# A two-layer decoder on one core: the order of VectorE and ScalarE at the beginnings and ends of feed-forward blocks

## The reference

```python
def swiglu(x, wgu, wd):
    gate, up = jnp.split(x @ wgu, 2, axis=-1)
    return (jax.nn.silu(gate) * up) @ wd

for i in range(DEPTH):                                   # DEPTH = 2
    h = h + 0.5 * swiglu(rms_norm(h, ffn1_norm[i]), ffn1_wgu[i], ffn1_wd[i])   # D_FF = 2816
    ...                                                  # mixing and cross attention
    h = h + 0.5 * swiglu(rms_norm(h, ffn2_norm[i]), ffn2_wgu[i], ffn2_wd[i])
return rms_norm(h, final_norm)
```

## Time and profile before

| | |
|---|---|
| median of 3 runs | 2177.72 us (2177.59 to 2182.73) |
| the profiled execution | 2179.78 us, its span 2177.8 us |
| TensorE busy | 2127.3 us, 98% |
| TensorE weight loads | 1855.7 us, 85% |
| VectorE busy | 1502.1 us, 69% |
| ScalarE busy | 907.6 us, 42% |
| GpSimd busy | 138.7 us, 6% |

### The profile page before, as it was taken

The page is one execution under the profiler, slowest core; times in us unless marked ns, Lnnn a source line. Parts: engine busy times, 40 slices in busy tenths (PEclk is TensorE's granted clock), DMA queues, the critical chain, the costliest instruction groups (busy, mean ns, idle before and its releaser), DMA issues. The chain is left out here.

```text
span 2177.8 us, 30026 instructions
## 1 busy us (share of the span) xinstructions
PE 2127.3 (98%) x12251; PEld 1855.7 (85%) x12251; DVE 1502.1 (69%) x2194; ACT 907.6 (42%) x1305; POOL 138.7 (6%) x114
## 2 busy tenths in 40 slices
PE   7999999999999999999989999999999999999998
PEld 6889888888888879888878888978888888888886
DVE  7777775657664787777577776756586457777775
ACT  6333433435434533334344433334464345334332
POOL 0000001100020200000110000021001102000001
PEclk9999999999999999999999999999999999999999
DMA  4333332422221233333223333343132212332331
GB/s 137 116 107 102 90 111 82 135 96 79 97 97 58 87 99 102 105 103 98 87 87 116 88 110 104 97 131 99 62 117 98 78 58 84 121 103 90 107 102 54
DMA packets 267940, 211.96 MB, mean 97 GB/s; under 512 B 7358, under 2 KB 234268, under 8 KB 267804
## 3 DMA queue, kind: packets, MB, share of 16 engines
q1 hardware_dynamic: 264544, 205.55, 30.3%
q10 hardware_dynamic: 3260, 4.51, 0.8%
HBM read 207.93 MB, written 2.10 MB: 96 GB/s over the span
## 5 line engine op out<-in xcount | busy, mean ns | idle before, releaser
L1804 PE MATMUL ps<-hid_hi,wn_hi 128*128 128x512 f32 x592 | 232.5, 393 | 2.5 <-DVE wn_lo L1355 1.8
L1805 PE MATMUL ps<-hid_lo,wn_hi 128*128 128x512 f32 x592 | 231.3, 391 | 0.0
L1806 PE MATMUL ps<-hid_hi,wn_lo 128*128 128x512 f32 x592 | 230.4, 389 | 0.0
L1366 DVE SCALAR_TENSOR_TENSOR h<-ps,h 128x512 f32<-128x512 f32 x224 | 148.3, 685 | 88.2 <-PE ps L1806 85.3
L1805 PE MATMUL ps<-hn_lo,wn_hi 128*128 128x512 f32 x448 | 175.2, 391 | 0.0
L1804 PE MATMUL ps<-hn_hi,wn_hi 128*128 128x512 f32 x448 | 175.1, 391 | 0.0
L1806 PE MATMUL ps<-hn_hi,wn_lo 128*128 128x512 f32 x448 | 174.2, 389 | 0.0
L638 ACT ACTIVATE w_hi<-raw 128x2048 fp32r<-128x2048 f32 x61 | 116.7, 1913 | 118.3 <-PE ps L1806 95.0
L1804 PE MATMUL ps<-hn_hi,w_hi 128*128 128x512 f32 x384 | 152.5, 397 | 3.5 <-DVE w_lo L1168 2.0
L780 ACT ACTIVATE wn_hi<-raw 128x768 fp32r<-128x768 f32 (+1 forms) x104 | 81.2, 806 | 170.8 <-PE ps L1806 170.8
L1805 PE MATMUL ps<-hn_lo,w_hi 128*128 128x512 f32 x384 | 150.7, 393 | 0.0
(11 more groups left out here) (323 smaller groups left out, 5897.7 us busy)
## 6 DMA issues: line engine op xcount, KB each, us to landing
raw<-in_ffn_wgu_dram SPq DMA_DIRECT2D x174, 512.0 KB, 4.8
raw<-in_ffn_wd_dram SPq DMA_DIRECT2D x48, 512.0 KB, 3.7
raw<-in_ffn_wd_dram SPq DMA_DIRECT2D x80, 256.0 KB, 3.7
raw<-in_w_in_dram SPq DMA_DIRECT2D x40, 512.0 KB, 4.4
raw<-in_cross_wkv_dram SPq DMA_DIRECT2D x32, 512.0 KB, 3.8
raw<-in_w_out_dram SPq DMA_DIRECT2D x16, 512.0 KB, 4.0
raw<-in_cross_wq_dram SPq DMA_DIRECT2D x16, 512.0 KB, 3.8
raw<-in_cross_wo_dram SPq DMA_DIRECT2D x16, 512.0 KB, 3.9
```

What stands on the lines that cost most here:

```text
L1366: dve.scalar_tensor_tensor(out=h[:, m, :], in0=ps[:, down_bank(c, m), :], scalar=0.5, in1=h[:, m, :], op0=ALU.mult, op1=ALU.add).then_inc( ...
L1804: pe.matmul(dst, a_hi, b_hi, start=start, stop=False)
L1805: pe.matmul(dst, a_hi, b_lo, start=False, stop=False)
L1806: return pe.matmul(dst, a_lo, b_hi, start=False, stop=stop)
```

## The change

It moves work on VectorE and ScalarE at both ends of the feed-forward blocks; no operation is added or left out. In a block's beginning the readouts of tiles 0 and 1 go ahead of the sums of pairs (tile 0 only in the first block, where it came behind pairs 0 and 1), N3's rounding and low part go behind tile 2's readout and between additions, and DB 0 is loaded ahead of N3. At a block's end the next stage's first unit is rounded and split ahead of squares and low parts, and each low part stands one addition later. In the last block TensorE asks for one scaled tile fewer before m = 6 and turns the one left out behind the last matmul. The down weights of chunk 1 get four places of their own (quarter_at), with other waits. One address of mg_lo moves by 128 bytes.

```diff
 def ffn_order():
-    order = [("N", 0), ("N", 1), ("N", 2), ("DA", 0), ("N", 3), ("DB", 0), ("S", 0), ("DA", 1)]
+    order = [("N", 0), ("N", 1), ("N", 2), ("DA", 0), ("DB", 0), ("N", 3), ("S", 0), ("DA", 1)]
...
+        def quarter_at(p, tiles):
+            return p * 512 if tiles == 2 else (p % 2) * 768
...  (ScalarE)
                 def down_round(c, p):
-                    if p < 2:
+                    if p < 2 or (c, p) == (1, 2):
                         act.wait_ge(wn_used, late_no(F, c + 2))
+                    elif c == 1:
+                        act.wait_ge(n_done, late_no(F, 3))
                     else:
                         act.wait_ge(d_done, d_no(F, c, 2 * p - 3))
...
                     round_third()
+                    whole_silu(0)
+                    whole_hid(0)
                 pair_scaled(0)
                 pair_scaled(1)
                 pair_rounded(0)
...
                     round_third()
                     copy_rb(rb_no, 7)
-                whole_silu(0)
-                whole_hid(0)
+                    whole_silu(0)
+                    whole_hid(0)
+                act.wait_ge(w_used, base + 4)
+                slot_round("DA", 0, 1, 1024)
+                whole_silu(1)
+                whole_hid(1)
                 pair_scaled(2)
                 pair_scaled(3)
                 pair_rounded(2)
                 pair_rounded(3)
-                act.wait_ge(w_used, base + 4)
-                slot_round("DA", 0, 1, 1024)
-                whole_silu(1)
-                whole_hid(1)
-                whole_round(3, 0)
-                whole_round(3, 1)
                 act.wait_ge(w_used, base + 5)
                 slot_round("DB", 0, 0, 1024)
                 whole_silu(2)
                 whole_hid(2)
+                whole_round(3, 0)
+                whole_round(3, 1)
...
+                if not final:
+                    round_next(0)
                 act.wait_ge(form_ready, 2 * fast_no(F, FAST - 1))
                 for m in range(KT):
...
-                    if m == 3 and not final:
-                        round_next(0)
...  (VectorE)
+                def first_hid():
+                    slot_low(3, "N", 2, 0, 2048)
+                    dve.wait_ge(rb_ready, L * 3 + (1 if f == 0 else 3))
+                    whole_gate(0)
+                    whole_scale(0)
+                    whole_product(0)
+                    whole_low(0)
                 if at_first:
-                    slot_low(3, "N", 2, 0, 2048)
+                    first_hid()
                 pair_made(0)
...
                 if not at_first:
-                    slot_low(3, "N", 2, 0, 2048)
-                dve.wait_ge(rb_ready, L * 3 + (1 if f == 0 else 3))
-                whole_gate(0)
-                whole_scale(0)
-                whole_product(0)
-                whole_low(0)
-                pair_made(2)
-                pair_made(3)
-                pair_low(2)
-                pair_low(3)
+                    first_hid()
                 whole_gate(1)
                 slot_low(4, "DA", 0, 1, 1024)
                 whole_scale(1)
                 whole_product(1)
                 whole_low(1)
-                whole_split(3, 0)
-                whole_split(3, 1)
+                pair_made(2)
+                pair_made(3)
+                pair_low(2)
+                pair_low(3)
                 whole_gate(2)
                 slot_low(5, "DB", 0, 0, 1024)
                 whole_scale(2)
                 whole_product(2)
                 whole_low(2)
-                for m in range(6):
-                    add_part(0, m)
+                add_part(0, 0)
+                add_part(0, 1)
+                whole_split(3, 0)
+                add_part(0, 2)
+                add_part(0, 3)
+                whole_split(3, 1)
+                add_part(0, 4)
+                add_part(0, 5)
                 form_sums(0)
...
                 add_last(0)
                 add_last(1)
+                if not final:
+                    split_unit(L, next_unit)
                 after_add(0)
-                add_last(2)
-                after_add(1)
-                after_add(2)
-                for m in range(3, KT):
+                for m in range(2, KT):
                     add_last(m)
-                    after_add(m)
-                    if m == 3 and not final:
-                        split_unit(L, next_unit)
+                    after_add(m - 1)
+                after_add(KT - 1)
...  (TensorE)
                         if final and m == 6:
-                            pe.wait_ge(hn_ready, hn_no(LAYERS, 0, 4))
-                            for j in range(5):
-                                for t in range(3 if j < 4 else 2):
+                            pe.wait_ge(hn_ready, hn_no(LAYERS, 0, 3))
+                            for j in range(4):
+                                for t in range(3 if j < 3 else 2):
                                     fin_turn(t, j)
                         if final and m == 7:
-                            pe.wait_ge(hn_ready, hn_no(LAYERS, 0, 5))
-                            fin_turn(2, 4)
+                            pe.wait_ge(hn_ready, hn_no(LAYERS, 0, 4))
+                            fin_turn(2, 3)
                             for t in range(3):
-                                fin_turn(t, 5)
+                                fin_turn(t, 4)
...
             last_tile = hn_no(LAYERS, 0, KT - 1)
+            pe.wait_ge(hn_ready, last_tile - 2)
+            for t in range(3):
+                fin_turn(t, KT - 3)
             pe.wait_ge(hn_ready, last_tile - 1)
```

## The result

| | before | after |
|---|---|---|
| median | 2177.65 us (2177.18 to 2182.73, 4 runs) | 2159.02 us (2158.46 to 2161.15, 4 runs) |
| the profiled execution | 2179.78 us, span 2177.8 | 2159.57 us, span 2157.6 |
| TensorE busy | 2127.3 us | 2120.6 us |
| VectorE busy | 1502.1 us | 1511.3 us |

The ratio is 0.9911 with a 95% interval of 0.9894 to 0.9928: 18.6 us less by the medians, 20.2 us less between the two profiled executions. The forecast was 2158.7 us, a gain of 19.0. By the interval the gain lies between 15.7 and 23.1 us; it is that wide because executions of the kernel before fall into two groups, here one at 2182.73 us and three near 2177.5, and beside the later runs on a second chip four of seven at 2182.4 to 2183.2 (mean granted clock 0.993) and three near 2177.7 (0.995).

The account below looks back on a forecast made before the run. TensorE was taken to be held by a few waits, mostly for VectorE, and by slow clock behind some. Gains of 6.9 + 0.2 + 6.1 + 5.0 + 0.75 = 19.0 us gave 2158.7 us from 2177.7, range 2154 to 2167.

Parts of the forecast that it names:

- Ends of blocks: Ends of blocks 1 and 3: both stalls for a unit's low part go, 3.05 us per end, gain 6.1 us.
- price of a stall: Anywhere on TensorE: a stall of x us idle costs x + 0.16 us.
- Rival 2: At block ends GpSimd and VectorE lock each other at 2.15 us a tile; gain 10.4 us, 2167 us; chance 0.12.
- End of block 2: First low-part stall goes, the token sums' wait falls to 1.0 us without cooling the clock; gain 5.0 us.
- Block 1: Beginning of block 1: stall moves to m = 4, 3.9 us long, slow clock 2.5; gain 0.2 us (-0.3 to +2.7).
- Beginnings of blocks 2 to 4: First chunk's m = 4 wait for h shrinks to 0.3 to 0.4 us each, a clock drop goes; gain 6.9 us.
- the 0.16s: At each TensorE stall: 0.16 us of cost added to its idle time.
- The very end: Last chunk's 1.37 us wait for scaled tile 4 goes, turns wait about 1.1 us; gain 0.75 us (0 to 1.5).
- Quarters: Down pieces of chunk 1 in places of their own: ScalarE freed earlier, TensorE's wait stays, nothing gained or lost.
- Rival 1: Block 1's moved stall doesn't cool the clock, GpSimd's sums are in time; gain 22.6 us, 2155 us; chance 0.15.
- Rival 3: Clock falls behind the short stalls that stay, at three places; 5 us back, 2163.8 us; chance 0.12.
- Rival 5: At three block ends the next unit's load comes late, needing 17.7 us against 4.4; 2184 us or more; chance 0.04.

Follow-up runs that it names:

- ahead_only: The changed kernel with each low part at the ends of blocks 1 to 3 directly behind its own addition again, unit split still ahead; 2171.01 us.
- short_squares: The changed kernel with GpSimd adding only 8 of 512 columns of each square, onto a preset sum; 2159.16 us in one execution.
- after_again: The changed kernel itself, unaltered, run and profiled again on a second chip; 2159.1 us.
- tile2_first: The changed kernel with DB 0 rounded behind tile 2's silu and its low part behind tile 2's product, in each block; 2157.57 us.
- pairs_late: The changed kernel with sums, rounding and low parts of pairs 2 and 3 moved behind add_part(0, 5) in all four blocks; 2167.44 us.
- no_quarters: The changed kernel with the down weights of chunk 1 in their old places and with the old waits; 2159.45 us.
- ends_only: The kernel before with only the change's edits at block ends and the very end; 2168.22 us against 2179.8, ratio 0.9944.
- begins_only: The kernel before with only the change's edits at block beginnings and the quarters; 2172.03 us, ratio 0.9961.

## Why the prediction was right, step by step

**Ends of blocks** (forecast 3.05 each, measured 3.3: the two stalls, 1.62 + 1.44 = 3.06, and 0.13 behind each). VectorE at the end of block 1:

```profile
361.65 2.28 DVE L1108 TENSOR_TENSOR w_lo<-raw,w_hi 128x2048 fp32r<-128x2048 f32 x1
363.85 1.78 DVE L1131 SCALAR_TENSOR_TENSOR hn_lo<-h,gains,hn_hi 128x512 fp32r<-128x512 f32 x1
365.56 0.68 DVE L1379 SCALAR_TENSOR_TENSOR h<-ps,h 128x512 f32<-128x512 f32 x1
366.16 1.18 DVE L1131 SCALAR_TENSOR_TENSOR hn_lo<-h,gains,hn_hi 128x512 fp32r<-128x512 f32 x1
...
375.49 3.29 DVE L1131 SCALAR_TENSOR_TENSOR hn_lo<-h,gains,hn_hi 128x512 fp32r<-128x512 f32 x2
378.70 2.28 DVE L1108 TENSOR_TENSOR w_lo<-raw,w_hi 128x2048 fp32r<-128x2048 f32 x1
```

The tiles follow each other every 1.7 to 2.1 us with low parts of 1.2 to 1.8, as laid out from the earlier trace rows. The forecast had the second split ready at 381.9 and wanted at 382.2; it was ready at 378.70 + 2.28 = 380.98 and wanted at 381.50. The margin is 0.5 us where 0.3 was forecast. The two times 0.13 were missing from the forecast's price of a stall: in before the first matmul behind each of these waits is followed by the next after 0.34 us and not 0.23 (372.90 to 373.24), and a few more lose hundredths. Rival 2 (a tile at 2.15 us) didn't come; ahead_only, with one move left out, shows how near it was. The Trainium skill's "SBUF — State Buffer" ("Who interferes with whom") states an exclusive lock on the ports that the two engines share, and that a VectorE instruction with two SBUF inputs, as these low parts are, contends with a GpSimd instruction that reads SBUF. The fall from 1409 to 747 ns in short_squares agrees.

**End of block 2** (forecast 5.0, measured 5.3). The sums waited 0.74 idle, 0.92 from start to start, where 1.0 was forecast, and the clock stayed full, as taken.

**Block 1** (forecast 0.2, measured 1.15). The stall moved from tile 1's low part to m = 4, as forecast, and was 3.63 us where 3.9 was written. The term that was mis-sized is the slow clock behind it: 3.4 us at half cost 1.6 us where I took 2.5, within the bounds given (0 to 3.0). The slow clock that goes had been sized too high by the same measure: a matmul at half took 0.43 us from start to start where 0.23 is usual, 0.20 more and not 0.23, so that 13 of them cost 2.6 us and not 3.0. In all 6.5 us went and 5.35 came back, against 6.65 and 6.4. And that the clock fell at all behind this stall is luck of the execution: behind 3.21 us it did in after_again and didn't in tile2_first. pairs_late shows that the pairs ahead of the addition are the cause of the stall.

**Beginnings of blocks 2 to 4** (forecast 6.9, measured 6.2). The mechanism was right; the main mis-sized term is what is left at m = 4: 0.54 us each, 1.6 in all, where I had 1.1 with the 0.16s. I took tile 2's readout at today's 4.44 us. It took 773.22 - 768.50 = 4.72, because it now starts together with ScalarE's rounding of DB 0 and waits for it. Today it starts 2.57 us of N3's split later, by when ScalarE is through. So the step missed that a readout moved up to the end of its own unit meets ScalarE there, though the same wait had been counted for tile 1. tile2_first took half of it back.

**The very end** (forecast 0.75, measured 1.1). The wait for scaled tile 4 is gone and the turns wait 0.85 idle behind the last product, 1.07 from start to start, for tile 6, as forecast (1.1).

**Quarters.** Nothing was forecast and nothing was measured, as no_quarters shows.

**What the sum did not have.** Setup lost 0.5 us between the two profiled executions and the mixing stages gave 0.35; neither is touched by the change. They nearly cancel, so they don't carry the agreement, but each is as large as the smaller terms of the sum. That the medians differ by 18.6 and the profiled executions by 20.2 comes from where they lie: the profiled one of before was 2.1 us above its median, that of after 0.5. So the closeness of 18.6 to 19.0 is in part luck. On the second chip the medians of the same two kernels differ by 23.3 us (2182.41 and 2159.1, ratio 0.9899). By place the terms miss by -0.7 to +0.95 us and partly cancel.

Rival 1 came neither in the clock nor in the sums. Rival 3 didn't come: no half clock stands in the profile of after between 65.3 us and the drain at 2150.8; that of after_again has one at 1554.0, in the mixing stages and not behind a stall that the change left. Rival 5, a late load, was not tried; no wait for a load stands at the ends of after.

## What to carry to other kernels

When an engine's order is changed, ask for each moved piece what filled the time that it leaves: the pairs filled 5.84 us of waiting for TensorE in three blocks and delayed TensorE in one. Moving them away won 3.1 us of stall there and cost 2.7 us at tile 3 in every block. A stall that goes must be followed to the next thing that is late; in block 1 it took back 5.35 of the 6.5 us that had gone. And two moves of one change may need each other: the split ahead without the later low parts was slower than both together by 11.9 us, and no better than neither. Last, a small gain is to be read by place: of tile2_first's 1.5 us only 0.8 was shown to come from what was changed.

## What was unexpected in the hardware

**The clock doesn't follow the length of a stall.** In ends_only the same wait stands in blocks 2 and 4, and only the second is followed by half clock:

```profile
776.44 0.47 PE L1802 MATMUL ps<-hid_hi,w_hi 128*128 128x512 f32 x1 [2.09 <-DVE h L1366]
...
1839.71 0.47 PE L1802 MATMUL ps<-hid_hi,w_hi 128*128 128x512 f32 x1 [2.08 <-DVE h L1366]
```

```profile
777.00:781.00 4.00, 4.00 (x19) 3.34 (x18) 3.33 (x5) 0.00 (x0) 0.00 (x0) 1.00 0.10 38
1840.30:1843.70 3.40, 3.40 (x10) 2.62 (x9) 1.75 (x3) 0.00 (x0) 0.00 (x0) 0.50 0.12 47
```

The same code behind the same 2.7 us wait for the sums had half clock for 3.4 us in before and for 6.8 us in begins_only (1096.1 to 1103.0), and the same 3.21 us wait had half clock behind it in after_again and full clock in tile2_first. A clock term of up to 3 us can therefore not be forecast from the stall, only bounded.

**Half clock can be partly free.** In the mixing stages of the first layer, before was at half clock, after at full:

```profile
497.90:501.30 3.40, 3.40 (x17) 3.40 (x18) 2.27 (x6) 3.37 (x7) 0.00 (x0) 0.51 0.00 0
```

```profile
493.90:497.30 3.40, 3.40 (x34) 3.27 (x34) 2.26 (x6) 3.37 (x7) 0.00 (x0) 1.00 0.00 0
```

The half clock (first fence, before) cost 1.55 us, but behind it two waits for ex, 0.60 and 0.73 us long by the starts, stand in after (second fence, the same work 4 us earlier) where the slow matmuls had covered them. ScalarE is busy for 3.37 of the 3.40 us in both and sets the pace there; the first ex was ready at 502.03 us in before and 498.02 in after, 4.0 apart, as the two executions were ahead of the half clock. The net was 0.3 us, nearly all of the mixing stages' 0.35. Half clock at the same place of the second layer cost after_again and short_squares 0.3 us each against after, too.
